# Hybrid decoder block: the modulated input made from a transposed x and per-partition columns, with three input chunks summed in the first stage

## The reference, cut to what matters

```
mod = silu(c) @ ada_w + ada_b                 # ada_w: 2048 x 12288
sh_a, sc_a, g_a, sh_f, sc_f, g_f = split(mod, 6)
h = rms_norm(x, attn_pre_g) * (1 + sc_a) + sh_a
proj = h @ w_in                               # 2048 x 7504
y = token_mixer(proj ...)                     # two attentions, gates, w_out
x = x + g_a * rms_norm(y, attn_post_g)
h = rms_norm(x, ffn_pre_g) * (1 + sc_f) + sh_f
y = peer_ffn(h)                               # gathers 128 rows of two tables for each token
x = x + g_f * rms_norm(y, ffn_post_g)
```

## Time and profile before

| | us |
|---|---|
| three runs, median (lowest to highest) | 2305.48 (2302.38 to 2306.29) |
| the profiled execution | 2303.61 |
| its span in the profile | 2301.8 |
| PE busy | 1973.8 (86%) |
| DVE busy | 1164.2 (51%) |
| POOL busy | 735.9 (32%) |
| ACT busy | 363.0 (16%) |

### The profile page before, as it was taken

The page is one execution under the profiler, slowest core; times in us unless marked ns, Lnnn a source line. Parts: engine busy times, 40 slices in busy tenths (PEclk is TensorE's granted clock), DMA queues, the critical chain, the costliest instruction groups (busy, mean ns, idle before and its releaser), DMA issues.

```text
span 2301.8 us, 15933 instructions
## 1 busy us (share of the span) xinstructions
PE 1973.8 (86%) x5203; PEld 908.4 (39%) x5203; DVE 1164.2 (51%) x2055; ACT 363.0 (16%) x954; POOL 735.9 (32%) x660
## 2 busy tenths in 40 slices
PE   1779899899989997999989888998677787778677
PEld 0335554344444443554434333443232333333233
DVE  6755214563341227777734344535556555555742
ACT  0001011112130113333401011111111011101101
POOL 2103000110000007565433223324644545454451
PEclk8789899999999999999999999999998888889889
DMA  9977745986679779999999999999999999999995
GB/s 348 363 258 269 288 121 173 321 311 232 243 281 346 284 242 417 422 421 421 421 418 417 418 417 419 418 417 421 422 422 420 420 422 422 422 413 422 422 421 245
DMA packets 163896, 828.56 MB, mean 360 GB/s; under 512 B 16660, under 2 KB 22984, under 8 KB 88180
## 3 DMA queue, kind: packets, MB, share of 16 engines
q0 software_dynamic: 91648, 637.57, 67.6%
q1 hardware_dynamic: 70084, 186.28, 22.6%
q10 hardware_dynamic: 2096, 3.85, 0.5%
HBM read 825.52 MB, written 2.13 MB: 360 GB/s over the span
## 4 chain that ended last, share of the span: by engine, by line
PE 50%; DMA 41%; DVE 5%; issue 2%; POOL 1%; ACT 1%; DVEq 0%; SPq 0%; POOLq 0%; ACTq 0%
DMA arena<-in_peer_v_dram,idx_now 23%; PE PS L1040 12%; PE PS L1501 12%; PE PS L1416 10%; PE PS L1459 9%; DMA arena<-in_ada_w_dram 7%; DMA arena<-in_w_out_dram 4%; DMA arena<-in_peer_w_q_dram 2%; DMA arena<-in_w_branch_mla_dram 2%; DVE arena L1611 2%; DVE arena L1557 2%; PE PS L1209 1%; DMA arena<-in_peer_u_dram,idx_now 1%; PE PS L1238 1%; DMA arena<-in_w_branch_nsa_dram 1%
## 5 line engine op out<-in xcount | busy, mean ns | idle before, releaser
L1501 PE MATMUL PS<-arena 128*128 128x512 f32 x1024 | 493.5, 646 | 142.9 <-DMA arena<-in_peer_v_dram,idx_now 142.9
L576 POOL DMA_INDIRECT arena<-in_peer_v_dram,idx_now x256 | 354.7, 1386 | 592.1 <-PE PS L1459 352.2
L1459 PE MATMUL PS<-arena 128*128 128x512 f32 x1024 | 472.1, 605 | 43.3 <-DMA arena<-in_peer_v_dram,idx_now 33.9
L2051 DVE CUSTOM_DVE_ANT_0 arena<-arena 128x2048 f32<-128x2048 f32 x128 | 291.8, 2291 | 243.8 <-DMA arena<-in_peer_u_dram,idx_now 243.7
L2025 DVE CUSTOM_DVE_ANT_0 arena<-arena 128x2048 f32<-128x2048 f32 x128 | 293.0, 2292 | 238.6 <-DMA arena<-in_peer_u_dram,idx_now 236.1
L1040 PE MATMUL PS<-arena 128*128 128x512 f32 (+1 forms) x912 | 399.7, 592 | 0.2 <-ACT arena L677 0.2
L1501 PEld LDWEIGHTS PS<-arena 128*128 128x128 f32 x1024 | 210.7, 208 | 425.7 <-issue 410.0
L1416 PE MATMUL PS<-arena 128*128 128x512 f32 x752 | 348.7, 606 | 27.5 <-DMA arena<-in_w_out_dram 14.0
L576 POOL DMA_INDIRECT arena<-in_peer_u_dram,idx_now x256 | 302.0, 1180 | 152.6 <-issue 70.1
L1459 PEld LDWEIGHTS PS<-arena 128*128 128x128 f32 x1024 | 191.2, 193 | 279.3 <-issue 225.2
L1040 PEld LDWEIGHTS PS<-arena 128*128 128x128 f32 x912 | 171.7, 193 | 189.8 <-issue 181.8
(11 more groups left out here) (254 smaller groups left out, 1133.1 us busy)
## 6 DMA issues: line engine op xcount, KB each, us to landing
arena<-in_ada_w_dram POOLq DMA_DIRECT2D x96, 1024.0 KB, 7.8
arena<-in_w_in_dram SPq DMA_DIRECT2D x112, 512.0 KB, 5.3
arena<-in_w_out_dram SPq DMA_DIRECT2D x64, 512.0 KB, 10.9
arena<-in_peer_w_q_dram SPq DMA_DIRECT2D x64, 512.0 KB, 7.5
arena<-in_w_branch_nsa_dram SPq DMA_DIRECT2D x32, 512.0 KB, 10.7
arena<-in_w_branch_mla_dram SPq DMA_DIRECT2D x32, 512.0 KB, 10.9
arena<-mod_rows SPq DMA_DIRECT2D x7, 1024.0 KB, 16.5
arena<-in_x_dram SPq DMA_DIRECT2D x4, 1024.0 KB, 9.3
```

Of the source, the lines that this page charges most:

```text
L576: pool.indirect_dma_start(dst, None, tab, bass.IndirectOffsetOnAxis(ap=idx_now[:, now, e:e + 1], axis=0)).then_inc(landed, 16)
L1459: ins = nc.tensor.matmul(PS[:, k, :], diag[i % 8], Vrow0[i % RING0][:, k * NC:(k + 1) * NC], start=(i == 0), stop=False, skip_group_check= ...
L1501: ins = nc.tensor.matmul(PS[:, 4 + k, :], diag[e % 8], Vrow[e % RING][:, k * NC:(k + 1) * NC], start=(first and e == 0), stop=False, skip_ ...
L2051: v.tensor_tensor_reduce(row, row, h2[1], 1.0, 0.0, ALU.mult, ALU.add, dots[:, e:e + 1]).then_inc(u_free, 1)
```

## The change

- x is multiplied by 1/rms on ACT as soon as that is known and stored as `x_tok`; PE transposes it in eight turns of four 128 x 128 blocks into eight PSUM banks and ACT copies these to `hT`.
- The bias (2 x 16 rows of 128) and the gain (16 rows) are loaded as rows of `cmp_rows`, which is now transposed once, before the first quarter; ACT copies the result to `mod_const` (columns) and `cmp_cols`. The three row broadcasts are gone.
- An ada tile now holds two rows of each partition for both segments, loaded by two DMAs of 512 KB. One partial sum for each segment, in two sets that alternate by quarter.
- PE multiplies 128 x 128 blocks of a partial sum, as the stationary operand, with one column of ones: eight products of one column each for a quarter. DVE adds the bias columns, forms (1 + scale) * gain, and applies both to `hT` in place, one `tensor_scalar` of 128 x 256 for each block of 128 of D.
- The first stage now accumulates three chunks (`MAIN[0]` to `MAIN[2]`) in banks 0 to 5, with six weight tiles for a quarter. Of each six, four are one block of D by 1024 columns, two are two blocks by 512 columns. The first eight wait for 2, 3, ... 9 finished ada tiles.
- Behind the stage PE's order is: chunk 3, transposes of `kdup`, chunk 4, compression products, chunk 5, value products of the compression, transposes of `k2dup`, tail. On DVE the three ropes come first, then eight ada rows, then the copies of the transposed keys.

```diff
@@ -331,11 +330,11 @@
-        CH_FIRST, QTRS = 2, D // NC
+        QTRS, FIRST_TILES = D // NC, 24
...
-        W_C2, W_C3, W_CMP, W_C4, W_C5, W_TAIL = 16, 24, 32, 40, 48, 56
+        W_C3, W_C4, W_CMP, W_C5, W_TAIL = 24, 32, 40, 48, 56
...
@@ -382,22 +381,23 @@
+        def first_acc(q, seg):
+            return acc[:, (2 * (q % 2) + seg) * NC:(2 * (q % 2) + seg + 1) * NC]
+        TURNS = [(q, t) for t in range(NT) for q in range(QTRS)]
+        def first_tile(m):
+            k4, i = 4 * (m // 6), m % 6
+            return (k4 + 2 * (i // 3), 2) if i % 3 == 2 else (k4 + i // 3 * 2 + i % 3, 1)
...
+                return r % 4, 16 * (KD + r // 4 + 1)
+            return r % 2, 16 * (KD + KD // 4 + (r - KD) // 2 + 1)
...
@@ -415,19 +415,24 @@
+            for m in range(FIRST_TILES):
+                k, n = first_tile(m)
+                if m < WSLOTS:
+                    sp.wait_ge(ada_used, 2 + m)
+                if n == 2:
+                    load(m, win_v[:, k:k + 2, MAIN[2] * NC:(MAIN[2] + 1) * NC])
+                else:
+                    if m >= WSLOTS:
+                        sp.wait_ge(w_used, m - WSLOTS + 1)
+                    sp.dma_start(wide[:, m % WSLOTS, :], win_v[:, k, MAIN[0] * NC:(MAIN[0] + 2) * NC]).then_inc(
+                        w_landed[m % WSLOTS], 16)
...
+            load_chunk(W_C4, MAIN[4] * NC)
...
@@ -502,12 +507,13 @@
-                q, seg, j = n // 8, n // 4 % 2, n % 4
...
-                pool.dma_start(ada_ring[:, n % ADA_SLOTS, :].rearrange("p (j n) -> p j n", j=4),
-                               ada_v[:, 4 * j:4 * j + 4, seg * D + q * NC:seg * D + (q + 1) * NC]).then_inc(
-                    ada_in[n % ADA_SLOTS], 16)
+                q, j = n // 8, 2 * (n % 8)
+                for k in range(2):
+                    pool.dma_start(ada_ring[:, n % ADA_SLOTS, 2 * k * NC:2 * (k + 1) * NC].rearrange("p (s n) -> p s n", s=2),
+                                   ada_v[:, j + k, 0:2 * D].rearrange("p (s n) -> p s n", s=2)[
+                                       :, :, q * NC:(q + 1) * NC]).then_inc(ada_in[n % ADA_SLOTS], 16)
...
@@ -637,13 +643,13 @@
-            act.dma_start(shift_row, ada_b[0, 0:D].partition_broadcast(P)).then_inc(first_rows_in, 16)
-            act.dma_start(scale_row, ada_b[0, D:2 * D].partition_broadcast(P)).then_inc(first_rows_in, 16)
-            act.dma_start(gain_row, attn_pre_g[0, :].partition_broadcast(P)).then_inc(first_rows_in, 16)
...
+            act.dma_start(cmp_rows[36:36 + 2 * KD, :], ada_b[0, 0:2 * D].rearrange("(k n) -> k n", n=P)).then_inc(small_in, 16)
+            act.dma_start(cmp_rows[36 + 2 * KD:36 + 3 * KD, :],
+                          attn_pre_g.rearrange("l (k n) -> (l k) n", n=P)).then_inc(small_in, 16)
...
@@ -651,23 +657,27 @@
-            def bank_out(n, dst):
+            root(1, RMS_X, NT)
+            act.wait_ge(xr_ready, 1)
+            for t in range(NT):
+                nc.scalar.activation(x_tok[:, t, :], X0[:, t, :], ACT.Copy, scale=rstd[:, t:t + 1]).then_inc(xn_ready, 1)
+            for n, (q, t) in enumerate(TURNS):
...
-                nc.scalar.copy(dst, PS[:, 4 + n % 4, :].rearrange("p (a b) -> p a b", b=P)).then_inc(tr_out[0], 1)
-            root(1, RMS_X, NT)
-            for n in range(0, TB_H, 2):
-                bank_out(n, hT[:, 2 * n:2 * n + 4, 0:P])
-            def chunk_out(n, used, dst, out_sem):
+                nc.scalar.copy(hT[:, 4 * q:4 * q + 4, t * P:(t + 1) * P],
+                               PS[:, n, :].rearrange("p (a b) -> p a b", b=P)).then_inc(tr_out, 1)
+            act.wait_ge(cmprow_in, 1)
+            nc.scalar.copy(mod_const.rearrange("p a b -> p (a b)"), PS[:, 7, 36:36 + 3 * KD])
+            nc.scalar.copy(cmp_cols[:, :], PS[:, 7, 0:36]).then_inc(cmpcols_ready, 1)
+            def chunk_out(n, used, dst, out_sem, bank=None):
...
-                    ins = nc.scalar.copy(d, PS[:, (n % 2) * 2 + t, 0:d.shape[-1]])
+                    ins = nc.scalar.copy(d, PS[:, ((n % 2) * 2 if bank is None else bank) + t, 0:d.shape[-1]])
...
-                chunk_out(n, used, lambda t: proj[:, t, MAIN[n] * NC:(MAIN[n] + 1) * NC], pj_out)
+                chunk_out(n, used, lambda t: proj[:, t, MAIN[n] * NC:(MAIN[n] + 1) * NC], pj_out, 4 if n == 2 else None)
...
@@ -681,10 +691,9 @@
-            for k in range(CH_FIRST):
-                main_out(k, CH_FIRST * 8 - 2 * (1 - k))
-            act.wait_ge(htok_ready, QTRS * NT)
-            act.wait_ge(tr_done, TB_H)
+            for n in range(3):
+                main_out(n, FIRST_TILES - (n < 2))
+            act.wait_ge(xn_ready, NT)
...
@@ -1059,44 +1057,49 @@
+            for n, (q, t) in enumerate(TURNS):
+                pe.wait_ge(xn_ready, t + 1)
+                for k in range(4):
+                    ins = nc.tensor.transpose(PS[:, n, k * P:(k + 1) * P], x_tok[:, t, (4 * q + k) * P:(4 * q + k + 1) * P],
+                                              ident[:, :])
+                ins.then_inc(tr_done, 1)
+            pe.wait_ge(tr_out, len(TURNS))
+            pe.wait_ge(small_in, 16 * 5)
+            rows_n = 36 + 3 * KD
+            nc.tensor.transpose(PS[:, 7, 0:rows_n], cmp_rows[:, :], ident[0:rows_n, 0:rows_n]).then_inc(cmprow_in, 1)
...
+                pe.wait_ge(ada_used, 8 * (q + 1))
...
+                    for k in range(4):
+                        c0 = 8 * q + 4 * seg + k
+                        ins = nc.tensor.matmul(PS[:, 6, c0:c0 + 1], first_acc(q, seg)[:, k * P:(k + 1) * P], ones[:, 0:1],
+                                               start=True, stop=True)
+                ins.then_inc(ada_cols, 1)
+                for m in range(6 * q, 6 * q + 6):
...
+                    k0, n = first_tile(m)
+                    pe.wait_ge(hT_ready, k0 + n)
+                    for t in range(NT):
+                        for i in range(2):
+                            kk, bank = (k0 + i, 4 + t) if n == 2 else (k0, 2 * i + t)
+                            ins = nc.tensor.matmul(PS[:, bank, :], hT[:, kk, t * P:(t + 1) * P], wring[:, m % WSLOTS, i, :],
+                                                   start=(kk == 0), stop=(kk == KD - 1))
...
+            pe.wait_ge(pj_out, 2)
+            chunk(2, W_C3, hT, KD)
...
+            pe.wait_ge(pj_out, 3)
...
+            chunk(0, W_C4, hT, KD)
...
@@ -1110,8 +1113,8 @@
-            pe.wait_ge(pj_out, 3)
-            chunk(0, W_C4, hT, KD)
+            pe.wait_ge(pj_out, 4)
+            chunk(2, W_C5, hT, KD)
...
@@ -1126,8 +1129,6 @@
-            pe.wait_ge(pj_out, 4)
-            chunk(2, W_C5, hT, KD)
...
@@ -1531,25 +1532,21 @@
-                ins = mean_square(RMS_X + t, X0[:, t, :], h_tok[:, t, :])
+                ins = mean_square(RMS_X + t, X0[:, t, :], x_tok[:, t, :])
...
-            inverse_root(1, RMS_X, NT)
+            dve.wait_ge(root_ready, 1)
+            v.reciprocal(rstd[:, RMS_X:RMS_X + NT], rstd[:, RMS_X:RMS_X + NT]).then_inc(xr_ready, 1)
...
-            def bank_out(n, dst):
-                dve.wait_ge(tr_done, n + 1)
-                v.tensor_copy(dst, PS[:, 4 + n % 4, :].rearrange("p (a b) -> p a b", b=P)).then_inc(tr_out[1], 1)
...
-                cols = slice(q * NC, (q + 1) * NC)
...
-                    dve.wait_ge(ada_in[n % ADA_SLOTS], 16 * (n // ADA_SLOTS + 1))
+                    dve.wait_ge(ada_in[n % ADA_SLOTS], 32 * (n // ADA_SLOTS + 1))
...
-                        j = 4 * (n % 4) + k
-                        part = first_acc(n // 4 % 2, k % 2)
+                        j, seg = 2 * (n % 8) + k // 2, k % 2
+                        part = first_acc(q, seg)
...
-                        if j >= 2:
+                        if j:
...
@@ -1559,22 +1556,18 @@
-                    if q and n == 8 * q:
-                        bank_out(2 * q - 1, hT[:, 4 * q - 4:4 * q, P:2 * P])
...
-                    dve.wait_ge(first_rows_in, 16 * 3)
-                for seg, row in enumerate((shift_row, scale_row)):
-                    dve.wait_ge(ada_cols, 2 * q + seg + 1)
-                    ins = v.tensor_tensor(row[:, cols], row[:, cols], PS[:, first_bank(q) + seg, :], ALU.add)
-                link(ins)
-                link(v.scalar_tensor_tensor(out=scale_row[:, cols], in0=scale_row[:, cols], scalar=1.0,
-                                            in1=gain_row[:, cols], op0=ALU.add, op1=ALU.mult))
-                for t in range(NT):
-                    link(v.scalar_tensor_tensor(out=h_tok[:, t, cols], in0=X0[:, t, cols],
-                                                scalar=rstd[:, RMS_X + t:RMS_X + t + 1], in1=scale_row[:, cols],
-                                                op0=ALU.mult, op1=ALU.mult))
-                    v.tensor_tensor(h_tok[:, t, cols], h_tok[:, t, cols], shift_row[:, cols], ALU.add).then_inc(htok_ready, 1)
-            bank_out(TB_H - 1, hT[:, KD - 4:KD, P:2 * P])
+                    dve.wait_ge(cmpcols_ready, 1)
+                    dve.wait_ge(tr_out, len(TURNS))
+                cols = slice(4 * q, 4 * q + 4)
```

(60 more changed lines are left out.)

44 lines of the change are left out of this document (13 added, 31 removed).

## The result

The changed kernel takes 2271.66 us (median of four runs, 2268.12 to 2277.3) against 2303.93 us of the kernel before beside it; the ratio is 0.9872 with a 95% interval of 0.9854 to 0.9891, 25 to 34 us less. A second set of five runs, taken with the last experiments, gave 2266.34 us and 0.9844 (0.9824 to 0.9864), 31 to 41 us less than the 2302.8 beside it. The forecast was 2270, range 2256 to 2284; its 35.2 us less lie just above the first interval and inside the second. Whole times of one kernel scatter by some 10 us between runs; so in what follows I read where stages end in the profiles, which for the changed kernel differ by about 1 us between its two profiles at the end of the last sum.

A forecast was written before the change was run, and what follows sets the result against it. The prediction took DMA bytes as the first stage's first bound and the pauses between quarters as the second. Its terms, -6.4 - 5.5 + 6.9 - 27.7 - 3 + 0.5, sum to -35.2: 2270 us, range 2256 to 2284.

The forecast's parts named there:

- item 1: Start: without the three row broadcasts x lands near 10.6 and the sums start at 15.6, 2.1 us earlier.
- item 2: End of the first stage's last ada sum: 137 instead of 143.5, 6.4 us earlier, bounds 125 and 144.
- the bytes bound of 132: End of the last ada sum if DMA never starves: last tile lands at 129, its sum gives 132.
- item 3: Hand-over from the last sum to TensorE's products: 4.4 us instead of 9.9, so -5.5.
- item 4: Last burst of products in the first stage: 48 passes instead of 32, +6.9 us.
- item 5: Third chunk no longer stands behind the first stage: -27.7 us.
- item 6: Order behind the stage: ada rows leave earlier, so the compression products' stall of 7.5 us shrinks by 0 to 5; -3.
- item 7: Compression's value products directly before the transposes that reuse their banks: one PSUM copy shows, +0.5 us.
- A: Rival: DMA runs at 410 GB/s, nothing starves, last sum at 125; -47, 2258 us; chance 0.12.
- B: Rival: third chunk's tiles eat the shorter pause's gain, last sum at 144; about -28, 2277 us; chance 0.15.
- C: Rival: TensorE's clock stays at 0.5 through the first stage's longer bursts; +32, 2337 us; chance 0.04.
- D: Rival: shift given back later, in a DMA-paced stretch or the attention's ada rows; half lost, 2288 us; chance 0.06.

The follow-up runs named there:

- the kernel with five additions: Changed kernel plus five 128x512 vector additions behind the modulation of each of the first three quarters; 2280.74 us, ratio 0.9928.
- the paced one with unused products: Changed kernel with ada rows 8 to 15 issued one at a time by weight-tile progress, plus nine unused TensorE products before the last hand-over; 2257.51 us, ratio 0.9821.

## Why the prediction was right, point by point

- Start (item 1): x landed at 9.9, not 10.6, and the sums started 2.9 us earlier, not 2.1.
- Last sum (item 2): forecast 137, measured 133.6. The 4 us that I left for starving did not occur; the bytes bound of 132 is nearly reached. What moved it by 9.9: the rows' bytes 7.2 (shown by putting them back) and the third chunk's tiles 5.7 the other way (shown by taking them out). The remaining 8.4 (9.5 by the second profile) I put down to the shorter pause, by difference; it is not shown as such, but putting a pause of the old length back cost 13.2 to 14.4.
- Hand-over (item 3): -5.2 for -5.5. The 16 passes took 3.59 for 3.5.
- Last burst (item 4): +7.4 for +6.9.
- The chunk (item 5): -27.7, as forecast. But the overlap pays in items 2 and 4: 27.5 less 7.2 in the burst and 5.7 at the last sum are the 14.6 it is worth.
- Order afterwards (item 6): the step that failed. Forecast -3, measured +1.2 (products of 26.6 instead of 25.4). The wait did end earlier against their start, at 12.7 instead of 18.3 us, as reckoned. I had not looked at which tile it would catch: the fifth instead of the seventh, so 64 passes stood behind it instead of 32, and after the idle time they ran at half clock (granted 0.50 from 231 to 244 us), 0.217 us each. The 5.6 us gained by the earlier end went there.
- Value products (item 7): nothing to see, for +0.5.
- The rest passed on: the first row sum of the attention comes 34.4 us earlier (346.4 for 380.8), the first product of the retrieval's second token tile (line 1501 before) 35.1, the end of the span 34.7. (In the second profile the first row sum comes 31.9 and the end 33.4 earlier.)

Sum measured: -9.9 - 5.2 + 7.4 - 27.7 + 1.2 is -34.2, and 0.2 us more are the transpose of `cmp_rows`, which left this place; together the 34.4 of the attention's start. The forecast had -35.2. Two terms (items 2 and 6) were off by some 3 to 4 us in opposite directions, so the total is nearer than its parts deserved; that is luck. Of the rivals: A did not occur, DMA carried 386 GB/s and the sum ended at 133.6 and not at 125. B's mechanism exists (5.7 us) but the rows' bytes paid for it. C did not occur, the long bursts ran at 0.43 us a pass but for their beginning. D's mechanism exists: the attention stretch that waits for ada rows was 6.0 us shorter in the kernel with five additions, whose stage ended later, and 4.1 longer in the paced one with unused products, whose stage ended earlier. That it passed the change's shift on whole is in part luck as well, for it was 78.0 us long before and 76.8 in this profile, but 74.1 in the second.

## What to carry to other kernels

In a stage that streams weights for a small serial step, count the bytes until its last tile first, then ask how long a pause of the consumer the ring covers; here four tiles of 1 MB nearly covered 5.5 us, and what was added to the pause up to 9 us was lost whole. Work that is moved under such a stage pays for its own bytes and for its share of the last burst: the 27.7 us of the third chunk were worth 14.6. Large prefetches issued together held back the small tiles of another queue at both places where they were put; issued one by one at the pace of those tiles they held nothing back, which was worth 12 to 17 us here. And before filling an idle engine to keep its clock up, see when the filler will end: here 2.7 of 4.0 us went to waiting for it.
